# Clearing the gated-recurrence buffers: seven memsets per layer moved from VectorE's program to GpSimd's

## The reference, cut to what matters

```
log_f = logaddexp(log(max(lbh, LB_FLOOR)), log1p(-lbh) + log_sigmoid(f_logit))
k = (1.0 - lbh) * sigmoid(-f_logit)
...
cb  = cumsum(lfc, axis=1)
dec = where(causal, exp(cb[q] - cb[k]), 0.0)
a   = einsum('bqhd,bkhd,bqkhd->bhqk', qc, kc, dec)
o   = einsum('bhqk,bkhe->bqhe', a, vc) + ...
```

## Time and profile before

| what | value |
|---|---|
| median of 3 executions | 2644.12 us (2643.14 to 2648.93) |
| the profiled execution | 2648.93 us |
| its span | 2647.0 us, mean granted clock 0.983 |
| PE / PEld busy | 2526.7 us (95%) / 2384.2 us (90%) |
| DVE / ACT busy | 1417.0 us (54%) / 1357.1 us (51%) |
| POOL busy | 1969.3 us (74%) |
| chain that ended last | PE 68%, POOL 14%, DVE 9%, ACT 4% |

### The profile page before, as it was taken

The page is one execution under the profiler, slowest core; times in us unless marked ns, Lnnn a source line. Parts: engine busy times, 40 slices in busy tenths (PEclk is TensorE's granted clock), DMA queues, the critical chain, the costliest instruction groups (busy, mean ns, idle before and its releaser), DMA issues.

```text
span 2647.0 us, 49411 instructions
## 1 busy us (share of the span) xinstructions
PE 2526.7 (95%) x19316; PEld 2384.2 (90%) x19316; DVE 1417.0 (54%) x2623; ACT 1357.1 (51%) x2369; POOL 1969.3 (74%) x2171
## 2 busy tenths in 40 slices
PE   9999999999999999999999989878889998998999
PEld 8989999999999888899999987778789998788999
DVE  7775443457537864343568454644345446755550
ACT  5444555556645344556466545451364445565543
POOL 8956668898889756569998985250169898566997
PEclk9999999999999999999999999899999999999999
DMA  7533434455565423345457653120046665333665
GB/s 218 144 95 98 120 112 142 130 168 168 165 185 148 125 80 112 112 127 154 139 173 208 192 157 100 56 72 1 13 119 196 179 178 148 88 96 105 199 189 154
DMA packets 683221, 354.91 MB, mean 134 GB/s; under 512 B 11152, under 2 KB 681072, under 8 KB 682608
## 3 DMA queue, kind: packets, MB, share of 16 engines
q1 hardware_dynamic: 680464, 343.45, 45.1%
q10 hardware_dynamic: 2528, 8.31, 0.9%
HBM read 350.67 MB, written 1.05 MB: 133 GB/s over the span
## 4 chain that ended last, share of the span: by engine, by line
PE 68%; POOL 14%; DVE 9%; ACT 4%; issue 2%; DMA 2%; ACTq 0%; DVEq 0%
PE pb L277 67%; POOL wl L346 14%; ACT pool L300 1%; ACT wh L335 1%; DMA raw<-in_w_ffn_in 1%; DVE pool L1122 1%; PE pb L554 1%; DVE bx L3375 0%; DVE pool L1108 0%; DVE pool L1136 0%; DMA raw<-in_ffn_w 0%; DMA raw<-in_w_in 0%; DMA raw<-in_w_ffn_out 0%; DVE pool L1107 0%; ACT pool L301 0%
## 5 line engine op out<-in xcount | busy, mean ns | idle before, releaser
L346 POOL TENSOR_TENSOR wl<-raw,wh 128x256 fp32r<-128x256 f32 (+1 forms) x2164 | 1961.8, 942 | 667.5 <-ACT wh L335 666.6
L277 PE MATMUL pb<-xh,wh 128*128 128x272 f32 (+2 forms) x3104 | 942.2, 304 | 24.8 <-DVE pool L1840 8.6
L335 ACT ACTIVATE wh<-raw 128x1024 fp32r<-128x1024 f32 (+2 forms) x669 | 690.5, 1034 | 450.2 <-PE pb L277 266.0
L277 PE MATMUL pb<-xl,wh 128*128 128x272 f32 (+2 forms) x3104 | 891.0, 287 | 0.0
L277 PE MATMUL pb<-xh,wl 128*128 128x272 f32 (+2 forms) x3104 | 890.6, 287 | 0.0
L277 PEld LDWEIGHTS pb<-xh,wh 128*128 128x128 f32 x3104 | 592.2, 191 | 49.1 <-issue 14.8
L277 PEld LDWEIGHTS pb<-xl,wh 128*128 128x128 f32 x3104 | 592.7, 191 | 3.9
L277 PEld LDWEIGHTS pb<-xh,wl 128*128 128x128 f32 x3104 | 592.1, 191 | 0.0
L277 PE MATMUL pb<-pool 128*128 128x128 f32 (+15 forms) x2048 | 311.5, 299 | 41.0 <-DVE pool L1136 7.4
L277 PEld LDWEIGHTS pb<-pool 128*128 128x128 f32 (+6 forms) x2048 | 239.8, 177 | 89.0 <-issue 23.4
L277 PE MATMUL pb<-u2h,wh 128*128 128x256 f32 x840 | 240.8, 287 | 2.5 <-DVE u2l L648 2.5
(11 more groups left out here) (392 smaller groups left out, 3775.9 us busy)
## 6 DMA issues: line engine op xcount, KB each, us to landing
raw<-in_w_in SPq DMA_DIRECT2D x208, 512.0 KB, 3.7
raw<-in_ffn_w SPq DMA_DIRECT2D x120, 512.0 KB, 4.1
raw<-in_w_ffn_in SPq DMA_DIRECT2D x88, 512.0 KB, 3.8
raw<-in_w_branch SPq DMA_DIRECT2D x48, 512.0 KB, 4.0
raw<-in_od_w_in SPq DMA_DIRECT2D x41, 512.0 KB, 3.8
raw<-in_w_ffn_out SPq DMA_DIRECT2D x32, 512.0 KB, 4.5
raw<-in_ev_w_in SPq DMA_DIRECT2D x20, 512.0 KB, 3.9
raw<-in_w_out SPq DMA_DIRECT2D x16, 512.0 KB, 4.0
```

The source lines that it names most:

```text
L277: return e.matmul(out, lhsT=l, rhs=r, start=a, stop=z, skip_group_check=True)
L335: E.e.activation(hi, src, ACT.Copy).then_inc(*sig("weight_hi", ("hi", g)))
L346: E.e.tensor_tensor(lo[:, s, :], src[:, s, :], hi[:, s, :].bitcast(F32), SUB).then_inc(*sig("weight_lo", *[("lo", g, i) for i in ks]))
```

## The change

DVE's `hgrn_prep` loses the list `cleared` and its memsets. POOL gets a generator `g_hgrn_prep` under the same name, so its steps are put into POOL's program during `hq` and `hi` at the same rate. It waits once for `hp_x` of the first pair of heads (DVE's first `held`), then clears the same seven buffers in the same order, one per step. Signals are left on those memsets for which something waits; the counts of `hg_zero` are now POOL's.

```
@@ v_hgrn_prep
-        cleared = [(x[half], (("hg_zero", li, half),) if x is AT2 else ()) for half in range(2) for x in (AT0, AT1, AT2)]
-        cleared += [(DV[:, 2, :], (("dv_pad", li),))]
         for u in range(14):
             hp, part = divmod(u, 3)
             if part == 0 and hp < 4:
                 held(hp)
-            if 1 <= u <= len(cleared):
-                e.memset(cleared[u - 1][0], 0.0).then_inc(*sig("hg_zero", *cleared[u - 1][1]))
             if part == 1 and hp:
                 sums(hp - 1)
@@ new
+    def g_hgrn_prep(E, li):
+        e = E.e
+        yield
+        e.wait_ge(*at("hp_x", li, 0))
+        for half in range(2):
+            e.memset(AT0[half], 0.0)
+            yield
+            e.memset(AT1[half], 0.0)
+            yield
+            e.memset(AT2[half], 0.0).then_inc(*sig("hg_zero", ("hg_zero", li, half)))
+            yield
+        e.memset(DV[:, 2, :], 0.0).then_inc(*sig("hg_zero", ("dv_pad", li)))
+        yield
@@ table of POOL's functions
-    GP = {"project": g_project, "begin": g_begin, "prime": g_prime, "rw_main": g_rw_main}
+    GP = {"project": g_project, "begin": g_begin, "prime": g_prime, "hgrn_prep": g_hgrn_prep, "rw_main": g_rw_main}
```

## The result

The changed kernel takes 2664.84 us in the median (2660.36 to 2668.27, 4 runs), the kernel before 2643.63 us beside it: ratio 1.0078, 95% interval 1.0053 to 1.0102. It is slower by some 21 us; +4.4 us was forecast, and the range ended at 2654.5 us. The profiled execution lies above these four, at 2673.06 us (span 2671.2); its span is 24.2 us above that of the profile before.

The account below looks back on a forecast made before the run. The prediction took POOL's unbroken subtractions in `hq` and `hi` to bound the kernel. 9.2 us of added memsets less 3.0 and 1.8 us returned gave +4.4 us, a median of 2648.5 us, range 2642.0 to 2654.5.

Parts of the forecast that it names:

- What bounds the kernel: In `hq` and `hi`, POOL's unbroken subtractions bound PE, 34.58 us in layer one and 63.02 in two; no memset is covered.
- Duration and place of the memsets: On POOL in `hq` and `hi`: 0.52, 0.95 and 1.01 us each, between the subtractions, 4.6 us a layer.
- the 1.1 us that I had named as a sign: POOL's memsets in `hq` and `hi`: the forecast would be wrong if they lasted over 1.1 us.
- What POOL gets back, and the sum: POOL in `hq` and `hi`: 9.2 us of memsets less 3.0 and 1.8 us returned, +4.4 us for both layers.
- The term of +4.4 us: Net time added to POOL's chain in `hq` and `hi` of both layers, and so to the kernel: +4.4 us.
- the two returns: POOL's subtractions: 3.0 us from DVE's memset pairs disappearing, 1.8 us from POOL's memsets not being stopped by DVE's reads.
- by itself this is worth nothing: Taking 4.78 us of memsets a layer from DVE saves nothing; DVE only waits longer for PE's results.
- DVE's 15.3 us of waits: Layer one's stretch: DVE waits 15.3 us for PE and ACT against 4.78 us of memsets, so DVE isn't the bound.
- PE's clock: Sign against the forecast: the granted clock falls where PE now waits longer; no time was put on it.
- Full price: Rival: POOL's returned waits come back elsewhere in `hq` and `hi`; +6.2 or +9.2 us, at most 10.1; chance 0.33.
- POOL is slower at it: Rival: POOL's memsets take twice DVE's 4.78 us a layer; +14.3 us, 2658.4 us; chance 0.03.
- DVE's time is what counts: Rival: DVE's queue sets when PE's results are taken over, so 9.56 us come off, 2634.6 us; chance 0.05.

Follow-up runs that it names:

- lead2: Changed kernel, but during `hi` POOL splits a piece only when PE is done with the piece two before (before: four): 2658.44 us, ratio 1.0060.
- both: Kernel before, DVE keeping its memsets, plus seven memsets a layer on POOL into unread scratch, same sizes and places: 2665.82 us, ratio 1.0081.
- copyzero: Changed kernel, but POOL clears the same buffers by copying a zero column in place of memsets: 2653.03 us, ratio 1.0045.
- act2: The program of `act` run once more, in more rounds: 2642.02 us against 2642.19 for the kernel before, ratio 1.0002.
- lead2b: Kernel before with the same wait on POOL during `hi` as `lead2`, as its control: 2640.33 us, ratio 0.9990.
- act: Neither DVE nor POOL clears; ACT writes the zeros at the same steps by seven copies of a zero column: 2637.41 us, ratio 0.9983.
- burst: Changed kernel with POOL's seven memsets in a row at the first place, in `hq`, none in `hi`: 2654.09 us, ratio 1.0049.

## Why the prediction was wrong

- **What bounds the kernel** held. POOL's chain covers the stretches, and none of the memsets was hidden.
- **Duration and place of the memsets** held, each within 0.01 us where nothing disturbed them. Some last longer beside DVE's tensor_scalar instructions: up to 1.30 us for 16 x 1088, over the 1.1 us that I had named as a sign, and 0.81 us for 512 columns. At 0.3 us each that is not the loss.
- **What POOL gets back, and the sum**: 2.0 us in layer one as forecast, 1.1 to 1.6 in place of 2.4 in layer two. The term of +4.4 us measured +3.1 to +3.6. The five subtractions of 1.46 to 2.30 us beside DVE's memsets are gone. I did not separate the two returns from each other by a run.
- **The step that failed** is "by itself this is worth nothing", with DVE's 15.3 us of waits as cover. I priced the contention between the two engines by the earlier trace rows, where they take turns and each loses one instruction of the other, and looked only for what POOL would lose or get back. What the runs showed instead: with memsets in POOL's row DVE is locked out for 19 or 20 subtractions in a row, the copy that PE needs next is queued behind, and the cover of at most 3.6 us at a time is gone. PE waits 10.0 and 10.5 us. My sum had no term for PE's clock either, though I had named it as a sign: standing that long brings it to 0.50, which adds 2.0 us. Together this is 12 us a layer, nearly three times my whole sum for both layers.
- **The loop that sets the length.** PE stands and waits for DVE, POOL goes on with the pieces that its lead allows, and DVE waits until POOL is about to run out: the instructions of over 12 us got their turn with POOL's third-last instruction of the row at the earliest, some only with its last or behind its end. `lead2` cuts the lead and with it wait and shift, 12.2 us to 4.0 in layer one and 12.3 to 8.4 in layer two, and its control costs nothing. So the lead bounds the long ones. It does not set the length of all: in these stretches the held instructions of 2.5 to 4.4 us, and the one of 7.46 us in `both`, ended with six or more POOL instructions still to come in the same row, and `lead2`'s 8.28 us with four.
- **The rivals.** *Full price* named a larger loss but not the mechanism, and its bound of +10.1 us was passed. *POOL is slower at it* comes nearest in time, 2658.4 us, but that would have been luck: its memsets, twice as long as DVE's, were not there (948 against 912 ns). In *DVE's time is what counts* I had asked where DVE stops waiting for PE, but thought only of a gain. The profile before had the warning, the row of 7.50 us at 2391 us, and the one of 7.26 us at 610 us; a list of instructions sorted by how far they exceed others of their form would have shown it.
- **What stays open**: why DVE loses its turn for many instructions. The Trainium skill (SBUF — State Buffer, section Who interferes with whom) has the pair of SBUF ports that the two engines share as a lock that whichever starts first holds for its whole instruction, while the other blocks. That fits the turns of the earlier trace rows, but does not account for a wait over 19 instructions of the other engine. Its rule that a GpSimd instruction that only writes does not contend with two-input VectorE instructions is compatible with what I counted: DVE comes up beside the memset, and the next subtraction takes the port (argued, not shown). But `copyzero` shows a case with a reading instruction, and `act2` and `lead2b` one with nothing added at all. What the cases have in common is a long POOL instruction or an undisturbed row of subtractions; which moment it takes besides was not settled, nor why `act` and `act2`, the same program, differ.

## What to carry to other kernels

Before a small job is moved to another engine, look at what it does to the turns that two engines take where they hold each other up, not only at its duration: here 4.6 us a layer of memsets in an unbroken row of POOL subtractions set PE back by 14 us a layer in the profiles (21 us in all by the medians), 12 of them from one VectorE instruction a layer that waited through nearly the whole row. An engine that runs in a row without waiting can hold up its neighbour for as long as its lead lasts; giving up lead that isn't needed (here two of four pieces, free of cost in the kernel before) bounds the damage. Count a long wait of PE at more than its length, since the clock can fall behind it. And in a profile, look for instructions that last many times the least of their form, also far from the change.

## What the runs showed of the hardware that I had not expected

- A VectorE instruction with inputs in SBUF can wait through nearly a whole row of GpSimd subtractions: 13.54 us for 0.7 us of work against 20 of them, 16.61 us at the most (`burst`). Two profiles of the changed kernel show it at the same two instructions, to 0.02 us; two profiles of `act`, again one program, do not agree on theirs.
- In most cases the two take turns, 1.2 us for each; 13 of 22 such instructions begun beside a GpSimd memset were locked out, 27 of 5640 beside its subtractions of 256 columns.
- GpSimd's memset of float32 is as fast as VectorE's: 948 ns against 912 for 1024 columns, and 998 against 965 for 16 partitions x 1088, so by the column 16 partitions cost as much as 128.
- The granted clock of TensorE was 0.50 from 100.0 to 110.2 us, after it had stood from 95.1 us for DVE, and a piece of 24 matmuls took 5.00 in place of 3.02 us.
